# Between output projection and FFN1: another order of the norm chain of each token tile, its transposes one product sooner, the first operands split under the last product

## The chip, the cores and the metric

The kernel runs on one core of a Trainium2 chip. The metric is the device time of one execution in microseconds (us). The engines are named as the profile names them: PE is TensorE, DVE is VectorE, ACT is ScalarE, POOL is GpSimd, SP is SyncE, which here only issues transfers.

## The reference

One decoder layer for 512 prompt tokens and 64 sample tokens, D_MODEL 1024, D_FF 2816. The change lies in the second half of it:

```
m = merged @ w_out                              # merged: the gated sum of both branches
h = x + rms_norm(m, norm_mix_post)
f = swiglu(rms_norm(h, norm_ffn_pre))           # swiglu(h): a, u = split(h @ w_ffn_in); silu(a) * u @ w_ffn_out
y = h + rms_norm(f, norm_ffn_post)

rms_norm(x, w) = x * rsqrt(mean(x * x) + EPS) * w
```

Everything is float32. A float32 product is made on PE of three passes over rounded operands, so each operand x is split: hi = round(x), done as a copy (on ACT or POOL), and lo = x - hi, done on DVE.

## The kernel before, in words

The program is written out by hand: each engine has its own function (`@block.tensor`, `@block.vector`, `@block.scalar`, `@block.gpsimd`, `@block.sync`) and runs its instructions in the order written. Semaphores alone tie them together. An engine that waits holds up all that stands behind the wait in its own order.

The 576 tokens are five tiles c: 0 to 3 of 128 tokens, and NC (number 4) of 64. The output projection makes m in two halves of 512 columns. Each half of a tile is 4 weight units (UB to UB+3 for the first half, UB+4 to UB+7 for the second) of 2 row blocks of 3 passes: 24 matmuls (`out_part`, L342). The second half of tiles 0 and 1 is nearly done beforehand, with one unit left for each; of tiles 2, 3 and NC all 24 are done in the loop over c.

Each tile then goes through a **norm chain** that passes three times between the engines:

- ACT `out_square(1, c)` (L1223): square of the second half and its sum along the row; then `root` (L1228, L1230) for 1/rms of m. Signals m_sq, then m_rms.
- DVE `half_gain(1, c)` (L1416) after m_sq, then after m_rms two instructions that give h (L1445, L1447). Signals m_half and h_s. Below, these three are called new h.
- ACT `h_square(c)` (L1240, then L1228, L1230): 1/rms of h. Signals h_rms.
- DVE `normed(c)` (L1421): the normed tile in the buffer hn, which has three places (c % 3). Signals hn_s.
- PE `turn(c)` (L1606): eight transposes into two PSUM banks. Signals h_turn.
- ACT `x_copy(c)` (L1246): copy to `mt`, features by tokens. Signals x_tok.

FFN1 is computed by Strassen's scheme on 2 x 2 blocks: seven products m1 to m7 for each of 22 column blocks i, each of 12 matmuls (`do_product`, L1662, 288 columns). Their left operands are quarters of the turned h (a11, a12, a21, a22) or sums of them: s1 = a21 + a22, s2 = s1 - a11, s3 = a11 - a21, s4 = a12 - s2. Tokens 0 to 287 are a11 and a12; 288 to 575 are a21 and a22. The first XM = 224 columns of a sum need tiles up to 3 only ("main"); the last 64 need tile NC ("rest"). Before the first product with an operand, ACT makes its hi part (L1250, L1277) and DVE its lo part (`operand_lo`, L1405). The hi and lo parts of a11 and a12 lie in the buffers x_hi and x_lo, over operands of the output projection. The right operands are weight groups g0 to g3; the first five are copied by POOL (L1208, list `FIRST`), of these (1, g0) and (0, g1) after the whole output projection, and get their lo parts on DVE (`group_lo`, L1390). `weight_sums(1)` (L1397, L1399, L1401) makes the weight sums of i = 1.

`PAIR_ORDER` sets the order of the products on PE. Products m1 and m2 of an i share a bank: m2 is added to m1 there, and it may start only when ACT `front(i)` (L1269) has copied m1 out. After the products, DVE adds the results up (L1480: `upper_sum`, `lower_sum`, `lower_right` and so on), and from there on PE, ACT and DVE go in step through the i.

The loop that the change touches on PE is, before:

```
            ins.then_inc(out_done, 1)
            if c >= 2:
                turn(c - 2)
        turn(3)
```

## Time and profile before

| what | value |
|---|---|
| median of 3 runs | 1115.4 us (1114.63 to 1115.46) |
| profiled execution, its own time | 1116.85 us |
| profiled execution, its span | 1115.1 us |
| mean granted PE clock | 0.991 |
| busy: PE, DVE, ACT, POOL | 1077.2, 685.7, 480.1, 52.2 us |
| the stretch that the change touches | about 680 to 731 us of the span |

The profile gives for each engine how long it was busy, and for each idle stretch before an instruction what ended it. Busy time of PE is nearly the whole span, so an idle stretch on PE is what can be won. A timeline row shows start, duration and instruction; instructions on one engine overlap by some hundredths to tenths of a us, so the step from one to the next is the distance of their starts.

### The profile page before, as it was taken

The numbers are of one execution on the slowest core, as the hardware profiler recorded it, in microseconds if no ns is written. First come the engines' busy times: TensorE is split into PE (matmuls) and PEld (weight loads), VectorE is DVE, ScalarE is ACT, GpSimd is POOL, SyncE is SP. The second block draws the span as 40 slices with busy tenths as digits, with TensorE's granted clock in tenths as the row PEclk, the third lists the DMA queues.
The fourth block names the chain that finished last, engine by engine and source line by source line (L and its number), as shares of the span: only waits on it lengthen the run. The fifth ranks groups of instructions, "written<-read, shape, count | busy, mean of one in ns | idle before, by whom it ended". The sixth has DMA issues, their size and how long they took to land.

```text
span 1115.1 us, 25037 instructions
## 1 busy us (share of the span) xinstructions
PE 1077.2 (97%) x10956; PEld 1013.4 (91%) x10956; DVE 685.7 (61%) x1001; ACT 480.1 (43%) x765; POOL 52.2 (5%) x78
## 2 busy tenths in 40 slices
PE   4999999999999999999999998789999999999998
PEld 4999999999999999999999877689999999988886
DVE  4246543566533756345755376799999999844544
ACT  4252244532435432446234444654444444533532
POOL 6000000100001000011000101000000000000000
PEclk9999999999999999999999998999999999999999
DMA  6522232522224522235222083032424242322212
GB/s 166 147 77 69 67 86 85 163 78 67 70 66 133 152 59 77 68 98 168 62 75 77 30 266 83 9 106 77 114 77 114 76 115 76 114 95 90 81 57 85
DMA packets 138620, 105.20 MB, mean 94 GB/s; under 512 B 3968, under 2 KB 123776, under 8 KB 138512
## 3 DMA queue, kind: packets, MB, share of 16 engines
q1 hardware_dynamic: 133648, 85.78, 26.9%
q0 software_dynamic: 4864, 17.83, 5.2%
q8 instruction: 87, 1.43, 0.5%
q14 instruction: 21, 0.17, 0.1%
HBM read 91.79 MB, written 11.80 MB: 93 GB/s over the span
## 4 chain that ended last, share of the span: by engine, by line
PE 91%; DVE 4%; ACT 1%; DVEq 1%; ACTq 1%; issue 0%; POOL 0%; DMA 0%; POOLq 0%
PE ps L253 43%; PE ps L1662 19%; PE ps L1684 13%; PE ps L342 4%; PE ps L934 2%; PE ps L988 2%; PE ps L965 1%; PE ps L955 1%; PE ps L911 1%; PE ps L967 1%; PE ps L972 1%; PE ps L948 1%; PE ps L981 1%; PE ps L974 1%; PE ps L930 0%
## 5 line engine op out<-in xcount | busy, mean ns | idle before, releaser
L253 PE MATMUL ps<-x_hi,w_lo_t 128*128 128x288 f32 x1168 | 256.6, 301 | 4.5 <-DVE w_lo_t L243 4.5
L253 PE MATMUL ps<-x_hi,w_hi_t 128*128 128x288 f32 x1168 | 250.5, 296 | 0.0
L253 PE MATMUL ps<-x_lo,w_hi_t 128*128 128x288 f32 x1168 | 250.5, 296 | 0.0
L239 ACT ACTIVATE w_hi_t<-w_raw_t 128x1024 fp32r<-128x1024 f32 x73 | 77.2, 1058 | 334.0 <-PE ps L253 322.2
L243 DVE TENSOR_TENSOR w_lo_t<-w_raw_t,w_hi_t 128x1024 fp32r<-128x1024 f32 x75 | 91.7, 1222 | 187.1 <-ACT w_hi_t L239 187.1
L253 PEld LDWEIGHTS ps<-x_hi,w_lo_t 128*128 128x128 f32 x1168 | 187.4, 189 | 9.5 <-DVE w_lo_t L243 4.6
L253 PEld LDWEIGHTS ps<-x_lo,w_hi_t 128*128 128x128 f32 x1168 | 188.7, 189 | 0.0
L253 PEld LDWEIGHTS ps<-x_hi,w_hi_t 128*128 128x128 f32 x1168 | 188.7, 189 | 0.0
L1662 PE MATMUL ps<-x_hi,w_lo_t 128*128 128x288 f32 x264 | 78.7, 298 | 5.6 <-issue 4.2
L1662 PE MATMUL ps<-x_lo,w_hi_t 128*128 128x288 f32 x264 | 78.4, 297 | 0.0
L1662 PE MATMUL ps<-x_hi,w_hi_t 128*128 128x288 f32 x264 | 78.3, 297 | 0.0
L1285 ACT ACTIVATE w_hi_t<-merged 128x1024 fp32r<-128x1024 f32 x41 | 43.1, 1055 | 57.0 <-PE ps L1662 49.2
L731 DVE TENSOR_TENSOR Q<-Q,B 128x768 f32<-128x768 f32 (+1 forms) x24 | 23.8, 992 | 69.6 <-PE ps L934 30.2
L1684 PE MATMUL ps<-w_hi_t,x_hi 128*128 128x512 f32 x180 | 57.1, 389 | 0.0
L1480 DVE TENSOR_TENSOR work<-work,ps 128x288 f32<-128x288 f32 x110 | 49.7, 452 | 11.9 <-PE ps L1662 7.6
L1662 PEld LDWEIGHTS ps<-x_hi,w_lo_t 128*128 128x128 f32 x264 | 50.0, 190 | 6.3 <-issue 5.2
L1390 DVE TENSOR_TENSOR w_lo_t<-merged,w_hi_t 128x1024 fp32r<-128x1024 f32 x43 | 52.3, 1221 | 0.9
L1662 PEld LDWEIGHTS ps<-x_hi,w_hi_t 128*128 128x128 f32 x264 | 50.2, 190 | 0.0
L1662 PEld LDWEIGHTS ps<-x_lo,w_hi_t 128*128 128x128 f32 x264 | 50.1, 190 | 0.0
L1509 DVE TENSOR_TENSOR w_lo_t<-w_raw_t,w_hi_t 128x1024 fp32r<-128x1024 f32 x17 | 20.8, 1224 | 44.0 <-ACT w_hi_t L1324 44.0
L810 DVE SCALAR_TENSOR_TENSOR h_t<-h_t,dec,ps 128x128 f32<-128x128 f32 (+1 forms) x96 | 30.5, 387 | 18.6 <-PE ps L988 18.6
L1324 ACT ACTIVATE w_hi_t<-w_raw_t 128x1024 fp32r<-128x1024 f32 x17 | 18.0, 1059 | 54.7 <-PE ps L1684 50.3
(282 smaller groups left out, 2126.5 us busy)
## 6 DMA issues: line engine op xcount, KB each, us to landing
w_raw_t<-in_w_in_dram SPq DMA_DIRECT2D x73, 512.0 KB, 3.6
merged<-in_w_ffn_in_dram SPq DMA_DIRECT2D x22, 512.0 KB, 5.1
w_raw_t<-in_w_ffn_in_dram SPq DMA_DIRECT2D x22, 512.0 KB, 4.5
w_raw_t<-in_w_ffn_out_dram SPq DMA_DIRECT2D x22, 512.0 KB, 3.6
h_t<-in_x_prompt_dram SPq DMA_DIRECT2D x8, 512.0 KB, 6.2
h_t<-in_state_gla_dram POOLq DMA_DIRECT2D x4, 1024.0 KB, 6.1
h_t<-in_state_hgrn_dram POOLq DMA_DIRECT2D x8, 512.0 KB, 8.2
out_dram<-h_t POOLq DMA_DIRECT2D x4, 1024.0 KB, 5.3
```

Of the source, the lines that this page charges most:

```text
L239: nc.scalar.activation(w_hi_t[:, u % NSPL, 0:nk, :], w_raw_t[:, u % NRAW, 0:nk, :], ACT.Copy).then_inc(w_hi, 1)
L243: nc.vector.tensor_tensor(w_lo_t[:, u % NSPL, 0:nk, :], w_raw_t[:, u % NRAW, 0:nk, :], w_hi_t[:, u % NSPL, 0:nk, :].bitcast(F32), ALU.subt ...
L253: m = nc.tensor.matmul(out[:, q, :], w[:, u % NSPL, k, :], x(k, q), start=first and i == 0, stop=last and i == len(todo) - 1)
L342: ins = pe.matmul(out_bank(half, c), x[:, k, cols], w[:, kk, :], start=first and i == 0, stop=last and i == 2, skip_group_check=True)
L731: dve.tensor_tensor(qf, qf, first.broadcast_to(shape), ALU.mult)
L810: ins = dve.scalar_tensor_tensor(st, st, dec[:, h, NC + b:NC + b + 1], s[:, o:o + w], ALU.mult, ALU.add)
L934: m = nc.tensor.matmul(s[t:t + STRIP, o + t // 2:o + (t + STRIP) // 2], K[:, h, c * C + t:c * C + t + STRIP], second(Q[:, h, c * C + t:c * ...
L1285: act.activation(group(i, g, True), group_raw(i, g), ACT.Copy).then_inc(g_hi, 1)
L1390: dve.tensor_tensor(group(i, g, False), group_raw(i, g), group(i, g, True).bitcast(F32), ALU.subtract).then_inc(first_lo if (i, g) in FIRS ...
L1480: return dve.tensor_tensor(out, term, bank(i, m), ALU.add)
L1662: ins = nc.tensor.matmul(bank(i, m), w[:, k0 + k, :], xx[:, k, :], start=(k == 0 and n == 0 and m in STARTS), stop=(k == 3 and n == 2), sk ...
L1684: m = nc.tensor.matmul(f_bank(half, t), x, w, start=first and i == 0, stop=last and i == len(todo) - 1)
```

## The change

Nothing is computed that was not computed before, but for one instruction: ACT's copy for the hi part of s2 is made in two (main and rest). What changes is the order on three engines.

- PE: `turn(1)` and `turn(2)` both stand before the products of tile NC, `turn(3)` behind product (0, m1), `turn(NC)` behind (1, m1). In PAIR_ORDER (0, m2) now comes ahead of (1, m1). The matmuls of units UB+4 and UB+5 of tile NC signal a new semaphore x_free, since after them x_hi and x_lo of a11 and a12 are free.
- DVE: new h of tiles 0 and 1 come first, then `normed` of both; `group_lo(0, "g3")` and `weight_sums(1)` stand behind tiles 2 and 3; the lo parts of a11 and a12 are made ahead of new h of tile NC; s3 is made whole and after the lo part of s2; s4 after it.
- ACT: the roots and squares of tiles follow that order; the hi parts of a11 and a12 wait for x_free and stand ahead of tile NC's root.

```diff
--- before.py
+++ after.py
@@ -74,7 +74,7 @@
 PRODUCTS = {"m1": ("a11", "b11"), "m2": ("a12", "b21"), "m3": ("s4", "b22"), "m4": ("a22", "t4"),
             "m5": ("s1", "t1"), "m6": ("s2", "t2"), "m7": ("s3", "t3")}
 TURN = ("m1", "m6", "m7", "m5", "m2", "m4", "m3")
-PAIR_ORDER = ([(0, "m1"), (1, "m1"), (0, "m2"), (1, "m2")] + [(i, m) for i in (0, 1) for m in TURN if m not in ("m1", "m2")]
+PAIR_ORDER = ([(0, "m1"), (0, "m2"), (1, "m1"), (1, "m2")] + [(i, m) for i in (0, 1) for m in TURN if m not in ("m1", "m2")]
               + [(i, m) for i in range(2, FT) for m in TURN])
 PRODUCT_NO = {im: r for r, im in enumerate(PAIR_ORDER)}
 BANK = {"m1": 0, "m2": 0, "m5": 1, "m3": 1, "m6": 2, "m7": 3, "m4": 3}
@@ -1091,6 +1091,8 @@
     g_hi = sem("g_hi")
     g_lo = sem("g_lo")
     a_hi = sem("a_hi")
+    s_main = sem("s_main")
+    x_free = sem("x_free")
     s_rest = sem("s_rest")
     xs_hi = sem("xs_hi")
     xs_lo = sem("xs_lo")
@@ -1249,19 +1251,6 @@
             act.drain()
             act.activation(operand(x, True), x_raw[x], ACT.Copy).then_inc(a_hi, 1)
 
-        for i in range(NT):
-            if i >= 1:
-                h_square(i - 1)
-            if i >= 2:
-                x_copy(i - 2)
-            out_square(1, i)
-            root(i, part[0:tok(i), 1, i:i + 1], stat[0:tok(i), 0, i:i + 1], m_rms)
-        first_x_hi("a11")
-        h_square(NC)
-        x_copy(3)
-        first_x_hi("a12")
-        x_copy(4)
-
         def front(i):
             act.wait_ge(product, PRODUCT_NO[i, "m1"] + 1)
             if i >= 2:
@@ -1291,9 +1280,35 @@
                 act.wait_ge(act_s, i)
             act.activation(fs, fa[:, i % 2, :], ACT.Sigmoid).then_inc(sig_s, 1)
 
+        def h_root(c):
+            out_square(1, c)
+            root(c, part[0:tok(c), 1, c:c + 1], stat[0:tok(c), 0, c:c + 1], m_rms)
+
+        h_root(0)
+        h_root(1)
+        h_square(0)
+        h_square(1)
+        h_root(2)
+        x_copy(0)
+        h_square(2)
+        h_root(3)
+        x_copy(1)
+        x_copy(2)
+        h_square(3)
+        act.wait_ge(x_free, 1)
+        first_x_hi("a11")
+        act.wait_ge(x_free, 2)
+        first_x_hi("a12")
+        h_root(NC)
+        x_copy(3)
         front(0)
+        h_square(NC)
         front(1)
-        sum_hi(1, "s2")
+        x_copy(4)
+        act.wait_ge(s_main, 1)
+        act.activation(operand("s2", True)[:, :, 0:XM], sums["s2"][:, :, 0:XM], ACT.Copy)
+        act.wait_ge(s_rest, 1)
+        act.activation(operand("s2", True)[:, :, XM:HT], sums["s2"][:, :, XM:HT], ACT.Copy).then_inc(xs_hi, 1)
         sum_hi(2, "s3")
         sum_hi(1, "s1")
         act.activation(operand("a22", True), x_raw["a22"], ACT.Copy).then_inc(xs_hi, 1)
@@ -1425,20 +1440,16 @@
         dve.wait_ge(st_out, 80 * G)
         for c in range(NT):
             half_gain(0, c, m_half0[0:tok(c), c, :], m_zero)
-        group_lo(0, "g3")
-        dve.drain()
-        weight_sums(1)
-        for c in range(NT):
-            n, back = tok(c), hn[0:tok(c), c % 3, HALF:D]
-            if c == NC:
-                back = hn[0:n, 1, HALF:D]
-            if c >= 1:
-                normed(c - 1)
+
+        def second_sum(c):
+            n = tok(c)
+            return hn[0:n, c % 3, HALF:D]
+
+        def new_h(c):
+            n, back = tok(c), second_sum(c)
             if c >= 3:
                 dve.wait_ge(h_turn, c - 2)
             half_gain(1, c, back, m_half)
-            if c == NC:
-                group_lo(1, "g0")
             dve.wait_ge(h_in[c], 16)
             dve.drain()
             dve.wait_ge(m_rms, c + 1)
@@ -1446,34 +1457,47 @@
                                      ALU.mult, ALU.add)
             dve.scalar_tensor_tensor(h_t[0:n, c, HALF:D], back, stat[0:n, 1, c:c + 1], h_t[0:n, c, HALF:D],
                                      ALU.mult, ALU.add).then_inc(h_s, 1)
-            if c == 0:
-                dve.wait_ge(g_pre_in, 16)
-
+
+        def x_sum(x, a, op, b, cols):
+            return dve.tensor_tensor(sums[x][:, :, cols], a[:, :, cols], b[:, :, cols], op)
+        main, rest, whole = slice(0, XM), slice(XM, HT), slice(0, HT)
+
+        new_h(0)
+        new_h(1)
+        dve.wait_ge(g_pre_in, 16)
+        normed(0)
+        normed(1)
+        new_h(2)
+        group_lo(0, "g3")
+        normed(2)
+        new_h(3)
+        dve.drain()
+        weight_sums(1)
+        normed(3)
         dve.wait_ge(a_hi, 1)
         operand_lo("a11")
-        normed(NC)
         dve.wait_ge(a_hi, 2)
         operand_lo("a12")
-        main, rest = slice(0, XM), slice(XM, HT)
-
-        def x_sum(x, a, op, b, cols):
-            return dve.tensor_tensor(sums[x][:, :, cols], a[:, :, cols], b[:, :, cols], op)
+        new_h(NC)
+        group_lo(1, "g0")
+        normed(NC)
         dve.wait_ge(x_tok, NC)
-        for cols in (main, rest):
-            if cols == rest:
-                dve.wait_ge(x_tok, NT)
-            x_sum("s1", x_raw["a21"], ALU.add, x_raw["a22"], cols)
-            dve.drain()
-            s2 = x_sum("s2", sums["s1"], ALU.subtract, x_raw["a11"], cols)
-            s3 = x_sum("s3", x_raw["a11"], ALU.subtract, x_raw["a21"], cols)
-        s2.then_inc(s_rest, 1)
-        s3.then_inc(s_rest, 1)
+        dve.drain()
+        x_sum("s1", x_raw["a21"], ALU.add, x_raw["a22"], main)
+        dve.drain()
+        x_sum("s2", sums["s1"], ALU.subtract, x_raw["a11"], main).then_inc(s_main, 1)
         group_lo(0, "g1")
-        for k, x in enumerate(("s2", "s3", "s1")):
-            dve.wait_ge(xs_hi, k + 1)
+        dve.wait_ge(x_tok, NT)
+        x_sum("s1", x_raw["a21"], ALU.add, x_raw["a22"], rest)
+        dve.drain()
+        x_sum("s2", sums["s1"], ALU.subtract, x_raw["a11"], rest).then_inc(s_rest, 1)
+        dve.wait_ge(xs_hi, 1)
+        operand_lo("s2")
+        x_sum("s3", x_raw["a11"], ALU.subtract, x_raw["a21"], whole).then_inc(s_rest, 1)
+        dve.tensor_tensor(sums["s4"], x_raw["a12"], sums["s2"], ALU.subtract).then_inc(s_rest, 1)
+        for k, x in enumerate(("s3", "s1")):
+            dve.wait_ge(xs_hi, k + 2)
             operand_lo(x)
-            if x == "s3":
-                dve.tensor_tensor(sums["s4"], x_raw["a12"], sums["s2"], ALU.subtract).then_inc(s_rest, 1)
 
         def add_up(i, m, out, term):
             dve.wait_ge(product, PRODUCT_NO[i, m] + 1)
@@ -1634,10 +1658,14 @@
             for u in range(UB + 7 if c < 2 else UB + 4, UC):
                 for kk in range(2):
                     ins = out_part(nc.tensor, u, c, kk, u == UB + 4 and kk == 0, kk == 1)
+                if c == NC and u < UB + 6:
+                    ins.then_inc(x_free, 1)
             ins.then_inc(out_done, 1)
-            if c >= 2:
-                turn(c - 2)
-        turn(3)
+            if c == 2:
+                turn(0)
+            if c == 3:
+                turn(1)
+                turn(2)
 
         def do_product(i, m):
             x, b = PRODUCTS[m]
@@ -1666,6 +1694,8 @@
         for i, m in PAIR_ORDER:
             do_product(i, m)
             if (i, m) == (0, "m1"):
+                turn(3)
+            if (i, m) == (1, "m1"):
                 turn(NC)
 
         def tile(n, t, kks, first, last):
```

PE at the turns and the first product of FFN1 (ident is the identity matrix, so those rows are the transposes; each opening row of a product is shown). Before, in the order of the program, and each row once:

```order
L1606 MATMUL ps<-ident,a 128x128 [waits hn_s]
L1606 MATMUL ps<-ident,a 128x128 x7
L1606 MATMUL ps<-ident,a 128x128 [waits x_tok,hn_s]
L1606 MATMUL ps<-ident,a 128x128 x7
L1662 MATMUL ps<-x_hi,w_lo_t 128x288 [waits x_tok,m_half,xs_lo,first_lo]
L1662 MATMUL ps<-x_lo,w_hi_t 128x288
```

and with the change, between the products of tile 3 and those of tile NC:

```order
L342 MATMUL ps<-xe_hi,x_hi 128x512
L1630 MATMUL ps<-ident,a 128x128 [waits hn_s]
L1630 MATMUL ps<-ident,a 128x128 x7
L1630 MATMUL ps<-ident,a 128x128 [waits hn_s]
L1630 MATMUL ps<-ident,a 128x128 x7
L342 MATMUL ps<-xe_lo,x_hi 128x512 [waits m_zero]
```

Before, turn(2) and turn(3) stood between tile NC's products and (0, m1). Now turn(1) and turn(2) stand ahead of tile NC's products, and (0, m1) follows those at once.

DVE from the first half's gains on, before:

```order
L1416 TENSOR_TENSOR work<-ps,a 64x512 [waits m_sq]
L1390 TENSOR_TENSOR w_lo_t<-merged,w_hi_t 128x1024 [waits first_hi]
L1397 TENSOR_TENSOR merged<-w_raw_t 128x1024 [waits pair_raw1]
L1399 TENSOR_TENSOR merged<-w_raw_t,merged 128x512
L1401 TENSOR_TENSOR merged<-w_raw_t,merged 128x512
L1416 TENSOR_TENSOR a<-ps,a 128x512 [waits m_sq]
L1445 SCALAR_TENSOR_TENSOR h_t<-work,stat,h_t 128x512 [waits h_in0,m_rms]
L1447 SCALAR_TENSOR_TENSOR h_t<-a,stat,h_t 128x512
L1421 SCALAR_TENSOR_TENSOR a<-h_t,stat,a 128x1024 [waits h_rms,g_pre_in]
```

and with the change:

```order
L1431 TENSOR_TENSOR work<-ps,a 64x512 [waits m_sq]
L1431 TENSOR_TENSOR a<-ps,a 128x512 [waits m_sq]
L1456 SCALAR_TENSOR_TENSOR h_t<-work,stat,h_t 128x512 [waits h_in0,m_rms]
L1458 SCALAR_TENSOR_TENSOR h_t<-a,stat,h_t 128x512
L1431 TENSOR_TENSOR a<-ps,a 128x512 [waits m_sq]
L1456 SCALAR_TENSOR_TENSOR h_t<-work,stat,h_t 128x512 [waits h_in1,m_rms]
L1458 SCALAR_TENSOR_TENSOR h_t<-a,stat,h_t 128x512
L1436 SCALAR_TENSOR_TENSOR a<-h_t,stat,a 128x1024 [waits h_rms,g_pre_in]
L1436 SCALAR_TENSOR_TENSOR a<-h_t,stat,a 128x1024 [waits h_rms]
```

The four weight instructions no longer stand ahead of tile 0, and tile 1's new h is done while ACT makes tile 0's root.

DVE from tile 3's last step to the lo part of s3, with the change (before, the lo part of a12 stood behind normed(NC), and all six sums ahead of the first lo part):

```order
L1436 SCALAR_TENSOR_TENSOR a<-h_t,stat,a 128x1024 [waits h_rms]
L1420 TENSOR_TENSOR x_lo<-a,x_hi 128x1152 [waits a_hi] x2
L1431 TENSOR_TENSOR a<-ps,a 64x512 [waits m_sq,h_turn]
L1456 SCALAR_TENSOR_TENSOR h_t<-work,stat,h_t 64x512 [waits h_in4,m_rms]
L1458 SCALAR_TENSOR_TENSOR h_t<-a,stat,h_t 64x512
L1405 TENSOR_TENSOR w_lo_t<-w_raw_t,w_hi_t 128x1024 [waits first_hi]
L1436 SCALAR_TENSOR_TENSOR a<-h_t,stat,a 64x1024 [waits h_rms]
L1462 TENSOR_TENSOR a<-a 128x4x224 [waits x_tok]
L1462 TENSOR_TENSOR a<-a 128x4x224
L1405 TENSOR_TENSOR w_lo<-merged,w_hi 128x512 [waits first_hi]
L1462 TENSOR_TENSOR a<-a 128x4x64 [waits x_tok]
L1462 TENSOR_TENSOR a<-a 128x4x64
```

Both lo parts (one row, x2) now come ahead of tile NC, and one sum fewer stands ahead of the rest sums in each part.

## Rows read from the trace of the kernel before

**Rows 1.** The page, its part 1, the engines over the whole span
```profile
PE 1077.2 (97%) x10956; PEld 1013.4 (91%) x10956; DVE 685.7 (61%) x1001; ACT 480.1 (43%) x765; POOL 52.2 (5%) x78
```

**Rows 2.** Engines by stretch of 2 us: busy time, then PEclk, DMA share, GB/s
```profile
690.00:692.00 2.00, 1.85 (x9) 1.85 (x10) 1.91 (x4) 0.00 (x0) 0.00 (x0) 0.50 0.02 4
...
714.00:716.00 2.00, 2.00 (x10) 2.00 (x10) 1.28 (x1) 1.90 (x2) 0.00 (x0) 0.50 0.00 0
...
722.00:724.00 2.00, 0.35 (x3) 0.11 (x1) 1.70 (x3) 2.00 (x3) 0.00 (x0) 1.00 0.04 11
```

**Rows 3.** Timeline, PE: start us, us, line, instruction, [idle before <- releaser]
```profile
686.31 0.40 PE L342 MATMUL ps<-xe_hi,x_hi 128*128 128x512 f32 x1
...
690.15 1.97 PE L1606 MATMUL ps<-ident,a 128*128 128x128 f32 x8 [3.44 <-DVE a L1421]
...
699.37 1.03 PE L1606 MATMUL ps<-ident,a 128*128 128x128 f32 x8
...
705.83 1.03 PE L1606 MATMUL ps<-ident,a 128*128 128x128 f32 x8
...
708.23 1.09 PE L1606 MATMUL ps<-ident,a 128*128 128x128 f32 x8 [1.36 <-DVE a L1421]
...
713.55 0.58 PE L1662 MATMUL ps<-x_hi,w_lo_t 128*128 128x288 f32 x1 [4.23 <-issue]
...
724.38 0.37 PE L1662 MATMUL ps<-xe_hi,w_lo_t 128*128 128x288 f32 x1 [2.04 <-issue]
...
730.54 0.37 PE L1662 MATMUL ps<-x_hi,w_lo_t 128*128 128x288 f32 x1 [0.52 <-DVE work L1480]
```

**Rows 4.** The chain of waits in order of time, its piece from 754.49 us (asked up to 810 us)
```profile
754.49 55.54 PE ps L1662 x417
```

**Rows 5.** Timeline, ACT: the norm chain, the copies, the first halves
```profile
679.76 0.60 ACT L1223 ACTIVATE a<-ps 128x512 f32<-128x512 f32 x1 [1.03 <-PE ps L342]
...
680.26 0.19 ACT L1223 ACTIVATION_READ_ACCUMULATOR a<-ps 128x1 f32 x1
...
680.90 0.20 ACT L1230 ACTIVATE stat<-stat 128x1 f32<-128x1 f32 x1
...
686.92 1.06 ACT L1240 ACTIVATE a<-h_t 128x1024 f32<-128x1024 f32 x1 [5.82 <-DVE h_t L1447]
...
693.92 1.00 ACT L1246 ACTIVATE a<-ps 128x1024 f32<-128x1024 f32 x1
...
715.13 1.16 ACT L1250 ACTIVATE x_hi<-a 128x1152 fp32r<-128x1152 f32 x1
...
717.88 0.40 ACT L1269 ACTIVATE work<-ps 128x288 f32<-128x288 f32 x1
```

**Rows 6.** Timeline, DVE: from the weight sums to the first product sum
```profile
681.87 1.23 DVE L1397 TENSOR_TENSOR merged<-w_raw_t 128x1024 f32<-128x1024 f32 x1
...
684.69 0.69 DVE L1416 TENSOR_TENSOR a<-ps,a 128x512 f32<-128x512 f32 x1
...
688.81 1.28 DVE L1421 SCALAR_TENSOR_TENSOR a<-h_t,stat,a 128x1024 f32<-128x1024 f32 x1 [1.92 <-ACT stat L1230]
...
706.27 1.90 DVE L1421 SCALAR_TENSOR_TENSOR a<-h_t,stat,a 128x1024 f32<-128x1024 f32 x1 [1.85 <-ACT stat L1230]
...
716.32 1.36 DVE L1405 TENSOR_TENSOR x_lo<-a,x_hi 128x1152 fp32r<-128x1152 f32 x1 [1.01 <-ACT x_hi L1250]
...
728.12 0.46 DVE L1480 TENSOR_TENSOR work<-work,ps 128x288 f32<-128x288 f32 x1
```

**Rows 7.** Groups of DVE instructions, shapes apart, 716 to 732 us
```profile
L1460 DVE TENSOR_TENSOR a<-a 128x896 f32<-128x896 f32 x3 | 3.2, 1087 | 0.1
...
L1460 DVE TENSOR_TENSOR a<-a 128x256 f32<-128x256 f32 x3 | 1.2, 421 | 0.1
```

**Rows 8.** Timeline, POOL: its two copies after the output projection
```profile
706.06 1.04 POOL L1208 CAST w_hi_t<-w_raw_t 128x1024 fp32r<-128x1024 f32 x1 [32.70 <-PE ps L342]
...
707.04 1.60 POOL L1208 CAST w_hi<-merged 128x512 fp32r<-128x512 f32 x1
```

## The prediction

> **What bounds the kernel now.** I read the page first: PE is busy 1077.2 of 1115.1 us [rows 1], so time can be won only where PE stands idle or runs at the lower clock. Next the timeline of PE around the change. It shows five holes [rows 3]: 3.44 us ahead of turn(0) at 690.15, 1.36 ahead of turn(3) at 708.23, 4.23 ahead of (0, m1) at 713.55, 2.04 ahead of (0, m6) at 724.38, and 0.52 ahead of (0, m4) at 730.54. That is 11.6 us. Then the windows for the clock: after the first and the third hole the granted clock is 0.50, the lower level of 1.2 GHz [rows 2]. After the hole of 2.04 us it was still 1.00 [rows 2]. Last, the timelines of ACT and DVE tell what each hole waits for. PE is not short of work there: it waits for the norm chain of a tile, which DVE (weight sums first) and ACT hand to and fro. From 754.49 us on PE runs on without a hole [rows 4], so a shift of all engines that lasts until there lasts to the end.
>
> **The change, part by part.** All times are on the span of the profiled execution.
>
> *Turn(0).* PE is through tile 2's products at 686.55 (686.31 and one step of 0.24) and stands until 690.15 [rows 3], because DVE did the weight sums from 681.87 on and came to tile 0's new h only at 684.69 [rows 6]. Its new h takes until 686.92, 2.23 us with the hand-over, and the root and the next start on DVE come 1.89 later, at 688.81 [rows 5, 6]. With the change DVE has no weight work ahead. ACT's square of tile 0 starts at 679.76, its row sum is there at 680.45 and its root at 681.10 [rows 5]. So new h of tile 0 runs from 680.5 to 682.8, that of tile 1 until 684.9 (its root, 1.34 behind the same product order, is there at 682.5), and normed(0), 1.28 long, ends at 686.1. ACT is through with tile 0's root of h at 684.6. Turn(0) starts at once at 686.55, with 0.4 us to spare. The hole of 3.44 us goes, and with it the slow stretch behind it.
>
> *Tile 3.* A turn and the 24 matmuls of a tile at full clock are 705.83 - 699.37 = 6.46; the turn's share is about 0.8 (1.03 less the overlap with the next) [rows 3]. Tile 3 is done at 686.55 + 6.46 = 693.0; before it was 699.4. PE has gained 6.4 us there. Turn(1) and turn(2) follow without a wait: normed(2) ends at about 693.4 by the same steps, turn(2) is due at 693.8. Tile NC's products run 694.6 to 700.3.
>
> *From here DVE sets the pace.* It has nearly no idle time in the following sum, which starts from tile 3's result at 693.15.
> - Row sum of the square: 0.69 [rows 5], with hand-over 693.95. New h(3): 2.23, to 696.2.
> - Weight sums: 2.82 (681.87 to 684.69) [rows 6], to 699.0. They were in front of tile 0 before; now (0, m1) waits for them.
> - normed(3): 1.20 (1.28 less the overlap with the next), to 700.2. ACT has tile 3's root long before, at 698.2 (behind two copies of 1.00 each [rows 5]).
> - Lo part of a11: 1.36 [rows 6], step 1.28, to 701.5. Its hi part on ACT is 1.16 [rows 5] and done at 699.4, since x_free came at 696.1. **(0, m1) starts at 701.6** instead of 713.55, after a hole of 1.3 us.
> - Lo part of a12: 1.28, plus POOL. POOL's copies for (1, g0) and (0, g1) come now at 700.4, when the output projection ends. Before, they met normed(3), which took 1.90 instead of 1.28 [rows 6], and POOL's own half-size copy took 1.60 [rows 8]. I take the 0.62 that DVE lost: to 703.4.
> - New h(NC) 2.2, to 705.6. The lo part of (1, g0) lies under ACT's root. The root is there 1.89 later, at 707.5. normed(NC), to 708.7.
> - s1 and s2 main: 1.09 each [rows 7], to 711.0. Lo part of (0, g1) 0.6. s1 and s2 rest 0.42 each [rows 7], with their waits to 712.4. ACT's rest copy, about 0.4 (as the 128x288 copy [rows 5]) to 712.9. Lo part of s2 1.36, to 714.3. **(0, m6) starts at 714.4** instead of 724.38.
> - s3 and s4: 1.27 each. Lo part of s3, to 718.2, **(0, m7) at 718.3**. Lo part of s1, to 719.5.
> - The first product sum starts on DVE at 719.5. Before, it was 728.12 [rows 6].
>
> On the POOL term the Trainium skill, page "SBUF — State Buffer", has a harder rule in its section "Who interferes with whom": a DVE instruction with two SBUF inputs and a GpSimd one exclude each other for the whole instruction. The trace agrees so far as normed(3) lost 0.62 to the end of a copy and the next copy lost about 1.1 to it; the rule's consequence here is a rival below.
>
> *What PE does meanwhile.* A product is 12 matmuls of 55.54/417 = 0.133 us [rows 4], 1.6 us. (0, m1) to 703.2, turn(3) to 704.0. Then (0, m2) needs ACT's copy of m1: ACT first copies tile 3 (1.00), then m1 (0.40) [rows 5], so PE waits about 1.6 us, to 705.7. This wait is new; before, (1, m1) lay there. (0, m2), (1, m1), turn(NC) and (1, m2) end at 711.3. Then a hole of 3.1 us before (0, m6), and one of 2.3 us after it before (0, m7), which is new too: before, s3 was ready together with s2. Holes are again some 8 us together. None of the holes of PE is on the path by itself, except as DVE is late. So the 12 us gained at (0, m1) shrink to 10 at (0, m6) and to 8.6 at the first product sum.
>
> *Behind it* the order of DVE and ACT is the same as before, and so are the sizes; PE's last three small holes up to 754.49 come from DVE, which is full there. The weight transfers for i = 2 start on the lo part of (0, g1), which is itself 10 us earlier. The shift passes on whole. The extra copy on ACT costs one start of an instruction and lies under DVE's work: nothing.
>
> *The sum.* 728.12 - 719.5 = 8.6. Adding up the kernel before with the same steps from 684.69 gives 726.9 for its 728.12: hand-overs are worth 1.2 more than I count. The stretch with the change has somewhat fewer of them, and I take 0.7. **The gain is 7.9 us.** Against the profiled execution: span 1115.1 - 7.9 = 1107.2, time 1116.85 - 7.9 = 1108.95. That execution was 1.45 above the median of the three runs, so for a median I say 1115.4 - 7.9 = **1107.5 us**. Without further mishap 1106.5 to 1108.5 (hand-overs 0 to 1.5, POOL 0 to 0.6).
>
> **The rivals.**
>
> *Both POOL copies block DVE whole.* The whole copy is 1.04 [rows 8], the one of half the size half of that, and both then stand in DVE's chain: 1.5 us instead of 0.62. For it: [rows 6, 8], where the two together took longer than each alone. Against: DVE's queue is full there, and POOL may be the one to wait, as at 707.04. Time 1108.4. That is also what the rule of the Trainium skill, page "SBUF — State Buffer", would make of it if POOL comes first both times.
>
> *The clock falls in the two holes before (0, m6) and (0, m7).* Before, 3.44 and 4.23 us of waiting were followed by 0.50 and 2.04 were not [rows 2, 3]; 3.1 and 2.3 with one product between lie in the middle. (0, m6) at half clock ends at 717.6, still ahead of 718.3. (0, m7) and (0, m5) lose 1.6 each as long as it lasts; DVE needs (0, m7) at 721.1 and (0, m5) at 722.7, so 0.1 to 2.5 of the 3.2 reach the path. Time about 1109, up to 1110.
>
> *Tile 0 misses its turn.* The margin is 0.4 us. If DVE or ACT lose a us or two on the first two tiles, the hole at turn(0) remains in part and the clock may go with it; the gain at tile 3 falls from 6.4 to some 3, and less weight work is hidden. Time 1110.5 to 1113. Against it: each step has a row.
>
> *More is kept.* If POOL costs nothing and the hand-overs are as short as I count, 1106; if besides the lo part of s3 comes without the wait on ACT's hi part, 1105.5.
>
> *Slower: the clock does not come back.* The new order has four holes (1.3, 1.6, 3.1, 2.3) with never more than some 6 us of work between. If the clock falls in the first and stays at 0.50 through (1, m7), that is 11 products at 3.2 instead of 1.6 and two turns, 19 us more of PE's time. Adding 3.2 per product and 1.6 per turn from 701.6 on, PE reaches (0, m4) at 728.4, still 2.1 ahead of before, for the new holes are then filled. (0, m4), (0, m3), (1, m6) and (1, m7) lose 6.4, so (1, m7) ends 4.3 later than before: about 1119. It decides from the point where the slow clock outlasts (0, m4). Against it: the clock that was at 0.50 at 690 gave a turn of 1.03 instead of 1.97 by 699.37, and turn(3), behind the hole of 1.36, took 1.09, the full-clock time [rows 2, 3].
>
> **How the numbers follow.** A measurement of this kernel can tell a difference of about 0.2%, 2.2 us. Forecast (1106.5 to 1108.5): 0.58. POOL blocks whole: 0.10. Clock falls in the pair of holes: 0.18. More kept: 0.05. Tile 0 misses its turn: 0.06, of which a third would end within 2.2 us of before. Slower: 0.03. So faster 0.95, same 0.02, slower 0.03. The range of 8 in 10 takes in the forecast, POOL and most of the clock case: 1105.9 to 1110.2.
>
> **What would show it.** Right: no hole on PE ahead of turn(0) and the clock at 1.00 from 688 to 700 us; (0, m1) at about 702 and waiting for the lo part of a11; new holes ahead of (0, m2) (released by ACT), (0, m6) and (0, m7) (by DVE); DVE without idle time from 694 to 719 but for three short waits; the first product sum at about 720. Wrong: a hole ahead of turn(0) or of turn(2); a clock of 0.50 anywhere from 700 to 725; a distance from (0, m4) to the end of the span that is not the 384.6 us of before [rows 3], which would mean that the shift is not passed on.

## The result, and the profile after

| | before | changed |
|---|---|---|
| median of 4 runs each, compared on one chip | 1115.43 us (1114.63 to 1116.64) | 1107.64 us (1106.44 to 1108.25) |
| ratio, with its 95% interval | | 0.9928 [0.9911, 0.9945] |
| profiled execution, span | 1115.1 us | 1105.5 us |

The change takes 7.8 us off. The forecast was 1107.5. The page shows no change of PE's share, only that its busy time fell by 4.9 us, from 1077.2 [rows 1], for the same number of matmuls (x10956); fewer of them ran at the lower clock. DVE has one instruction fewer, since s3 is made whole, and ACT one more, the second copy of s2:

```profile
PE 1072.3 (97%) x10956; PEld 1008.4 (91%) x10956; DVE 685.3 (62%) x1000; ACT 480.7 (43%) x766; POOL 53.1 (5%) x78
```

The spans differ by 9.6 us, not by 7.8. ACT's square of tile 0's second half, which lies ahead of anything that the change touches, starts at 679.76 before [rows 5] and here at 678.47, 1.29 us earlier. Starts of this instruction lie between 678.4 and 680.1 in all traces of this case, whatever the kernel, so that part is scatter of what runs ahead of it. I therefore measure from it: **D** is the distance from that start to the first product sum on DVE. It is 728.12 - 679.76 = 48.36 before [rows 5, 6] and 718.49 - 678.47 = 40.02 after, **8.34 less**. To compare single times with the forecast, add 1.29.

The timeline of PE after; it answers to [rows 3]:

```profile
685.25 1.03 PE L1630 MATMUL ps<-ident,a 128*128 128x128 f32 x8
...
691.70 1.91 PE L1630 MATMUL ps<-ident,a 128*128 128x128 f32 x16
...
700.34 0.37 PE L1690 MATMUL ps<-x_hi,w_lo_t 128*128 128x288 f32 x1 [1.15 <-issue]
...
702.01 1.03 PE L1630 MATMUL ps<-ident,a 128*128 128x128 f32 x8
...
704.55 0.37 PE L1690 MATMUL ps<-x_hi,w_lo_t 128*128 128x288 f32 x1 [1.51 <-ACT work L1258]
...
713.43 0.58 PE L1690 MATMUL ps<-xe_hi,w_lo_t 128*128 128x288 f32 x1 [3.03 <-issue]
...
717.29 0.37 PE L1690 MATMUL ps<-xe_hi,w_lo 128*128 128x288 f32 x1 [0.64 <-issue]
...
720.91 0.37 PE L1690 MATMUL ps<-x_hi,w_lo_t 128*128 128x288 f32 x1 [0.20 <-DVE work L1504]
```

There is no hole ahead of turn(0) (685.25), nor ahead of turn(1) and turn(2), which are one row of 16 transposes at 691.70. (0, m1) waits 1.15 us, (0, m2) 1.51, (0, m6) 3.03, (0, m7) 0.64. The last row is (0, m4): from its start to the end of the span it is 384.6 us (1105.5 - 720.91), as before.

The windows after: busy time of PE, PEld, DVE, ACT, POOL, then the granted clock, DMA share and GB/s:

```profile
688.00:690.00 2.00, 2.00 (x10) 1.64 (x9) 1.94 (x3) 1.15 (x2) 0.00 (x0) 1.00 0.02 4
...
702.00:704.00 2.00, 1.04 (x10) 0.81 (x8) 1.88 (x4) 0.92 (x1) 0.82 (x1) 1.00 0.00 0
...
714.00:716.00 2.00, 2.00 (x11) 2.00 (x10) 2.00 (x3) 1.36 (x2) 0.00 (x0) 0.50 0.90 236
...
718.00:720.00 2.00, 2.00 (x17) 2.00 (x16) 1.97 (x3) 1.55 (x3) 0.00 (x0) 1.00 0.00 0
```

After turn(0) the clock stays at 1.00, where it was 0.50 before [rows 2]. Between turn(0) and (0, m4) it is 0.50 once, from about 713.3 to 716.8 by windows of 1 us, from the end of the hole ahead of (0, m6) until (0, m6) is through.

The timeline of DVE after; it answers to [rows 6]:

```profile
683.48 1.28 DVE L1436 SCALAR_TENSOR_TENSOR a<-h_t,stat,a 128x1024 f32<-128x1024 f32 x1
...
690.66 1.28 DVE L1436 SCALAR_TENSOR_TENSOR a<-h_t,stat,a 128x1024 f32<-128x1024 f32 x1 [0.72 <-ACT stat L1232]
...
692.69 0.69 DVE L1431 TENSOR_TENSOR a<-ps,a 128x512 f32<-128x512 f32 x1 [0.75 <-ACT a L1225]
...
694.98 1.23 DVE L1412 TENSOR_TENSOR merged<-w_raw_t 128x1024 f32<-128x1024 f32 x1
...
697.69 1.28 DVE L1436 SCALAR_TENSOR_TENSOR a<-h_t,stat,a 128x1024 f32<-128x1024 f32 x1
...
698.89 3.46 DVE L1420 TENSOR_TENSOR x_lo<-a,x_hi 128x1152 fp32r<-128x1152 f32 x2
...
706.43 1.28 DVE L1436 SCALAR_TENSOR_TENSOR a<-h_t,stat,a 64x1024 f32<-64x1024 f32 x1 [0.72 <-ACT stat L1232]
...
711.97 1.36 DVE L1420 TENSOR_TENSOR xe_lo<-a,xe_hi 128x1152 fp32r<-128x1152 f32 x1 [0.48 <-ACT xe_hi L1311]
...
718.49 0.46 DVE L1504 TENSOR_TENSOR work<-work,ps 128x288 f32<-128x288 f32 x1
```

normed(0) starts at 683.48 instead of 688.81. From tile 3's half gain (692.69) on, DVE waits only for the root of tile NC (0.72 us at 706.43) and for the rest copy of s2 (0.48 us at 711.97). Two lo parts in one row take 3.46 us at 698.89, where 2.64 would be the step and duration of two of them. The answer for this line alone gives the duration of one, min, median and max in ns: the 2194 is the second of the pair, and it is the collision with POOL, below.

```profile
L1420 DVE TENSOR_TENSOR x_lo<-a,x_hi x4: 1350/1352/2194, 698.9 to 718.9; 128x1152 fp32r<-128x1152 f32 x4
```

ACT and POOL after; they answer to [rows 5] and [rows 8]:

```profile
678.47 0.60 ACT L1225 ACTIVATE a<-ps 128x512 f32<-128x512 f32 x1 [1.03 <-PE ps L342]
...
704.00 0.41 ACT L1258 ACTIVATE work<-ps 128x288 f32<-128x288 f32 x1
...
704.61 1.06 ACT L1242 ACTIVATE a<-h_t 64x1024 f32<-64x1024 f32 x1 [0.20 <-DVE h_t L1458]
```

```profile
699.25 1.89 POOL L1210 CAST w_hi_t<-w_raw_t 128x1024 fp32r<-128x1024 f32 x1 [27.42 <-PE ps L342]
...
701.09 1.73 POOL L1210 CAST w_hi<-merged 128x512 fp32r<-128x512 f32 x1
```

### The profile page after: what moved, and what is told of

The parts are those of the page before. It is cut to its first block, busy times and chain, and to the rows that moved or that the text cites. A ratio compares the mean times of both kernels' runs of the same rounds, so it can differ in the third digit from the quotient of the medians.

```text
span 1105.5 us, 25038 instructions
## 1 busy us (share of the span) xinstructions
PE 1072.3 (97%) x10956; PEld 1008.4 (91%) x10956; DVE 685.3 (62%) x1000; ACT 480.7 (43%) x766; POOL 53.1 (5%) x78
## 4 chain that ended last, share of the span: by engine, by line
PE 92%; DVE 4%; DVEq 1%; ACT 1%; POOL 0%; issue 0%; ACTq 0%; DMA 0%; POOLq 0%
PE ps L253 43%; PE ps L1690 20%; PE ps L1714 13%; PE ps L342 5%; PE ps L934 2%; PE ps L988 2%; PE ps L965 1%; PE ps L955 1%; PE ps L911 1%; PE ps L967 1%; PE ps L972 1%; PE ps L948 1%; PE ps L981 1%; PE ps L974 1%; PE ps L930 0%; POOL O L403 0%
## 5 line engine op out<-in xcount | busy, mean ns | idle before, releaser
L239 ACT ACTIVATE w_hi_t<-w_raw_t 128x1024 fp32r<-128x1024 f32 x73 | 77.3, 1058 | 333.7 <-PE ps L253 321.7
L1274 ACT ACTIVATE w_hi_t<-merged 128x1024 fp32r<-128x1024 f32 x41 | 43.1, 1055 | 57.0 <-PE ps L1690 49.2
L1690 PE MATMUL ps<-xe_hi,w_lo_t 128*128 128x288 f32 x128 | 38.5, 301 | 4.2 <-issue 3.0
```

Source lines behind the costliest of these rows:

```text
L239: nc.scalar.activation(w_hi_t[:, u % NSPL, 0:nk, :], w_raw_t[:, u % NRAW, 0:nk, :], ACT.Copy).then_inc(w_hi, 1)
L1274: act.activation(group(i, g, True), group_raw(i, g), ACT.Copy).then_inc(g_hi, 1)
L1690: ins = nc.tensor.matmul(bank(i, m), w[:, k0 + k, :], xx[:, k, :], start=(k == 0 and n == 0 and m in STARTS), stop=(k == 3 and n == 2), sk ...
```

## The experiments

All of them are measured by D and by a second distance. The hole on PE ahead of (2, m6), which DVE's lo part of a weight group ends, has the same 1.21 us in all traces. In the timeline of PE before and after it is this row:

```profile
744.94 0.40 PE L1662 MATMUL ps<-xe_hi,w_lo_t 128*128 128x288 f32 x1 [1.21 <-DVE w_lo_t L1390]
```

```profile
735.29 0.40 PE L1690 MATMUL ps<-xe_hi,w_lo_t 128*128 128x288 f32 x1 [1.21 <-DVE w_lo_t L1405]
```

From its end to the end of the span it is 370.1 to 370.3 us in all traces (1115.1 - 744.94 before, 1105.5 - 735.29 after). So, the scatter ahead of D aside, whatever a kernel wins or loses lies in D, or in the stretch between D's end and that matmul, called **S**. S is 16.82 before and 16.80 after. D and S come from one trace of each kernel. The ratio is to the kernel before as it ran beside each group of kernels (medians 1115.43, 1115.67, 1115.60 and 1115.33 us).

| kernel | D | S | median us | ratio to before, interval |
|---|---|---|---|---|
| before | 48.36 | 16.82 | 1115.4 | |
| changed | 40.02 | 16.80 | 1107.64 | 0.9928 [0.9911, 0.9945] |
| changed, again | 40.01 | 18.55 | 1108.90 | 0.9937 [0.9925, 0.9950] |
| weights later only | 43.89 | 16.81 | 1111.91 | 0.9964 [0.9950, 0.9978] |
| split late | 45.60 | 18.73 | 1114.87 | 0.9993 [0.9984, 1.0003] |
| split late, square first | 44.99 | 17.70 | 1113.07 | 0.9980 [0.9970, 0.9990] |
| old product order | 40.02 | 17.70 | 1108.29 | 0.9935 [0.9917, 0.9952] |
| sums whole | 39.84 | 16.82 | 1107.02 | 0.9922 [0.9906, 0.9938] |
| one more DVE instruction | 41.18 | 18.17 | 1110.83 | 0.9960 [0.9948, 0.9972] |
| weight sums last | 42.07 | 16.81 | 1110.43 | 0.9956 [0.9944, 0.9969] |
| fill | 39.43 | 16.80 | 1107.61 | 0.9930 [0.9918, 0.9942] |
| copies off POOL | 39.70 | 17.67 | 1108.32 | 0.9937 [0.9925, 0.9949] |
| three edits | 38.46 | 16.82 | 1106.34 | 0.9921 [0.9909, 0.9932] |
| three edits, sums split | 37.89 | 16.81 | 1105.75 | 0.9908 [0.9893, 0.9923] |

**Weights later only.** The kernel before, with one part of the change.

```diff
-        group_lo(0, "g3")
-        dve.drain()
-        weight_sums(1)
         for c in range(NT):
...
             if c == 0:
                 dve.wait_ge(g_pre_in, 16)
+            if c == 2:
+                group_lo(0, "g3")
+            if c == 3:
+                dve.drain()
+                weight_sums(1)
```

> The kernel before, with one part of the change alone: on VectorE the lo part of (0, g3) and the weight sums of i = 1 stand behind new h of tiles 2 and 3 instead of ahead of tile 0. I measure D, from the start of ACT's square of tile 0's second half to the first product sum on DVE (before 48.36 us, changed kernel 40.02 us). My theory (the hole at turn(0) comes from the weight work, and DVE paces the rest): no hole ahead of turn(0), no clock of 0.50 behind it, a new hole of some 2 to 3 us ahead of turn(3), (0, m1) some 6 us earlier than before, D about 42.4, time 6 us under the kernel before. Rival (the order of the turns and the early split carry most of the gain): D 45 to 47, time at most 3 us under before.

D fell by 4.47, a little over half of the change's 8.34. The hole ahead of turn(0) is gone. The timeline of PE shows two holes of another kind, ahead of turn(3) and of (0, m1):

```profile
703.77 1.97 PE L1608 MATMUL ps<-ident,a 128*128 128x128 f32 x8 [3.82 <-DVE a L1421]
...
708.56 0.58 PE L1664 MATMUL ps<-x_hi,w_lo_t 128*128 128x288 f32 x1 [2.82 <-issue]
```

The 3.82 us cost the clock as well: it was 0.50 from about 702.2 to 712.5 us, (0, m1) included. D lies between the two theories (42.4 and 45 to 47), and the median, 3.8 us under its kernel before (1115.67), between them too. What I had missed is POOL: its copies met the weight sums here, which took 1.23, 1.35 and 0.92 us instead of 1.23, 0.69 and 0.69. That is 0.89 of the 1.5 us above 42.4; the rest is not accounted for. So the order of the weights alone is worth somewhat more than half. The turns and the early split make up the rest, by difference: no run moves the turns by themselves.

**Split late.** The changed kernel, with the first operands split behind tile NC's root and new h again.

```diff
-        act.wait_ge(x_free, 1)
-        first_x_hi("a11")
-        act.wait_ge(x_free, 2)
-        first_x_hi("a12")
         h_root(NC)
+        act.wait_ge(x_free, 1)
+        first_x_hi("a11")
+        act.wait_ge(x_free, 2)
+        first_x_hi("a12")
...
-        dve.wait_ge(a_hi, 1)
-        operand_lo("a11")
-        dve.wait_ge(a_hi, 2)
-        operand_lo("a12")
         new_h(NC)
         group_lo(1, "g0")
+        dve.wait_ge(a_hi, 1)
+        operand_lo("a11")
+        dve.wait_ge(a_hi, 2)
+        operand_lo("a12")
```

> The changed kernel with a11 and a12 split late again: hi parts behind tile NC's root on ACT, lo parts behind new h(NC) and the lo part of (1, g0) on DVE. My theory: ACT's root of h(NC) stands behind its copy of (0, m1), so normed(NC) and all sums wait for (0, m1): (0, m1) starts 4 to 5 us later, D 44.0 instead of 40.02, time 4 us over the changed kernel. Rival (only the total of DVE's work between tile 3 and the first product sum counts, whatever its order): D 39.5 to 40.0, time the same.

D grew by 5.58, the time by 6 to 7 us (against the two medians of the changed kernel, 1108.90 and 1107.64). On PE the hole ahead of (0, m1) is 5.52 us, with the clock at 0.50 behind it (the first matmul 0.58 us long, as at 713.55 in [rows 3]):

```profile
706.02 0.58 PE L1690 MATMUL ps<-x_hi,w_lo_t 128*128 128x288 f32 x1 [5.52 <-issue]
```

and on DVE normed(NC) then waits 6.13 us for ACT's root of h, which stands behind ACT's copy of (0, m1):

```profile
713.31 1.28 DVE L1436 SCALAR_TENSOR_TENSOR a<-h_t,stat,a 64x1024 f32<-64x1024 f32 x1 [6.13 <-ACT stat L1232]
```

So the total of DVE's work is not what counts: DVE idles here. The miss of 1.6 against 44.0 is the clock. (0, m1) and turn(3) lie ahead of ACT's root of h(NC); from (0, m1) to turn(3) it was 3.01 instead of 1.67 us, and turn(3) took 1.22 instead of 1.03. The kernel lost this although it had one thing for free: POOL's two copies were through before the lo parts began (at 704.58), and these took 2.61 us instead of 3.46.

**Split late, square first.** As the last, with one more edit on ACT.

```diff
+        h_square(NC)
         x_copy(3)
         front(0)
-        h_square(NC)
```

> The kernel with the late split (D 45.60), and on ACT the square of h(NC) ahead of the copy of turned tile 3 and of (0, m1)'s copy. My theory (late splitting costs because PE's (0, m1) and turn(3) lie in the path of the sums, through ACT's order and through the copy of tile 3): normed(NC) comes 4 us earlier or more, but s1 main then waits for the copy of tile 3, which follows (0, m1); D 42.9. Rival (only the clock and the square's place cost): D 40 to 40.5.

The edit did what it says, and normed(NC) came early, at 706.78. But D fell by 0.61 only. The timeline of DVE shows where the wait went:

```profile
706.78 1.27 DVE L1436 SCALAR_TENSOR_TENSOR a<-h_t,stat,a 64x1024 f32<-64x1024 f32 x1
...
711.43 2.26 DVE L1462 TENSOR_TENSOR a<-a 128x896 f32<-128x896 f32 x2 [3.38 <-ACT a L1248]
...
716.51 0.93 DVE L1462 TENSOR_TENSOR a<-a 128x256 f32<-128x256 f32 x2 [2.22 <-ACT a L1248]
```

s1 main waits 3.38 us for the copy of turned tile 3, as expected, and then s1 rest waits 2.22 us for the copy of tile NC, which turn(NC) follows only behind (1, m1). I had forgotten the second. Both turns stand behind a product on PE; so long as (0, m1) is late, all sums are late. That is why mending ACT's order alone wins back so little. D is 2.1 above the 42.9 worked out, and most of this is the clock once more: from (0, m1) to turn(3) it was 3.02 us instead of 1.67, and turn(3) took 1.56 instead of 1.03, 1.9 us together. Without it D would be about 43.1, an estimate from these rows, which is what my theory gave, and far from the rival's 40 to 40.5.

**Old product order.** The changed kernel with PAIR_ORDER as before.

```diff
-PAIR_ORDER = ([(0, "m1"), (0, "m2"), (1, "m1"), (1, "m2")] + ...
+PAIR_ORDER = ([(0, "m1"), (1, "m1"), (0, "m2"), (1, "m2")] + ...
```

> The changed kernel with the old order of the first products: (0, m1), turn(3), (1, m1), turn(NC), (0, m2), (1, m2). My theory (DVE paces, PE's holes there are not on the path): the hole of 1.5 us ahead of (0, m2) goes and one of about 3 us ahead of (1, m1) comes, since its weights' lo part is late; (0, m6) starts at the same distance, D 40.0 within 0.2, time the same as the changed kernel. Rival (the order of the products is worth its hole): D 1.5 us away, either way.

D is 40.02 to the hundredth, though PE's holes moved: 2.71 us ahead of (1, m1) for its weights' lo part, 1.57 ahead of (0, m6), 2.04 ahead of (0, m7).

```profile
705.83 0.40 PE L1690 MATMUL ps<-x_hi,w_lo_t 128*128 128x288 f32 x1 [2.71 <-DVE w_lo_t L1405]
...
713.50 0.37 PE L1690 MATMUL ps<-xe_hi,w_lo_t 128*128 128x288 f32 x1 [1.57 <-issue]
...
717.36 0.37 PE L1690 MATMUL ps<-xe_hi,w_lo 128*128 128x288 f32 x1 [2.04 <-issue]
```

In D this part of the change is worth nothing by itself: the product order only chooses where PE waits. S is 17.70, 0.9 more than in the first trace of the changed kernel, with the clock at 0.50 from about 718.0 to 721.4, while (0, m7) and (0, m5) ran. Whether the order has a part in that is not shown, since S of the changed kernel itself differs by more than this between two traces.

**Sums whole.** The changed kernel with the sums and the hi part of s2 as before.

```diff
-        act.wait_ge(s_main, 1)
-        act.activation(operand("s2", True)[:, :, 0:XM], sums["s2"][:, :, 0:XM], ACT.Copy)
-        act.wait_ge(s_rest, 1)
-        act.activation(operand("s2", True)[:, :, XM:HT], sums["s2"][:, :, XM:HT], ACT.Copy).then_inc(xs_hi, 1)
+        sum_hi(1, "s2")
```

(and DVE's loop over main and rest of s1, s2, s3, as in the kernel before)

> The changed kernel with the sums as before: s1, s2, s3 main, then all three rest, and the hi part of s2 in one piece. My theory: (0, m6) starts about 1 us later, (0, m7) follows it without a hole, and D stays within 0.3 of 40.02, since DVE does the same work; time the same as the changed kernel. Rival (starting (0, m6) early is part of the gain): D and the time 1 to 2 us longer.

(0, m6) started 1.15 us later, (0, m7) without a hole, D 0.18 less. The finer cut of the sums brings nothing either; by trace it is a little worse.

**One more DVE instruction.** The changed kernel with s1 main computed twice.

```diff
         x_sum("s1", x_raw["a21"], ALU.add, x_raw["a22"], main)
+        dve.drain()
+        x_sum("s1", x_raw["a21"], ALU.add, x_raw["a22"], main)
```

> The changed kernel with s1 main computed twice: one more DVE instruction of 1.09 us, with its wait 1.2 us, ahead of (0, m6), at a place where PE has a hole of 3.0 us. My theory (DVE paces): D 41.2, time 1.2 longer. Rival (PE's holes have slack): D 40.0, time the same.

D grew by 1.16, by just the instruction and its wait. PE's hole ahead of (0, m6) grew by as much and gave nothing of it away:

```profile
715.45 0.58 PE L1692 MATMUL ps<-xe_hi,w_lo_t 128*128 128x288 f32 x1 [4.20 <-issue]
```

So DVE sets the pace from normed(NC) on. The median grew by 3.2 or 1.9 us (against 1107.64 and 1108.90), more than D, and S tells why: it is 18.17, 1.37 more, with the clock at 0.50 from about 713.5 to 723.7 (below).

**Weight sums last.** The changed kernel with `weight_sums(1)` behind the lo part of s1.

```diff
         new_h(3)
-        dve.drain()
-        weight_sums(1)
         normed(3)
...
             operand_lo(x)
+        weight_sums(1)
```

> The changed kernel with the weight sums of i = 1 (2.8 us of DVE) moved from ahead of normed(3) to behind the lo part of s1. My theory: in their old place they lie partly under ACT's root of tile 3 (DVE would idle some 2 us there), so (0, m1) starts only 0.8 us earlier, the 2.8 us come back later, and D grows by about 2, to 42.0; time 2 us over the changed kernel. Rival (they stand in the way of (0, m1), and what starts earlier there ends earlier): D 37.2, time 2.8 under it.

D 42.07, as worked out, 2 us worse. normed(3) waits for ACT's root of tile 3 in their stead:

```profile
698.16 1.28 DVE L1436 SCALAR_TENSOR_TENSOR a<-h_t,stat,a 128x1024 f32<-128x1024 f32 x1 [2.10 <-ACT stat L1232]
```

The place behind new h(3) is thus a good one: 2.1 of their 2.7 us lie under ACT's work.

**Fill.** The changed kernel with the lo part of (0, g1) in DVE's wait for the root of tile NC.

```diff
         group_lo(1, "g0")
+        group_lo(0, "g1")
         normed(NC)
...
         x_sum("s2", sums["s1"], ALU.subtract, x_raw["a11"], main).then_inc(s_main, 1)
-        group_lo(0, "g1")
```

> The changed kernel with the lo part of (0, g1) moved on DVE into its wait of 0.72 us ahead of normed(NC). My theory (DVE paces from tile 3 to the first product sum, so filled idle time is time won): D 39.4 instead of 40.02, time 0.6 us shorter, which the runs can hardly tell but the trace can. Rival (PE paces): D unchanged.

D 39.43: 0.59 won, as expected, and not to be told in the medians.

**Copies off POOL.** The changed kernel; POOL makes its copy for (0, g1) with its first ones, and ACT that for (1, g0).

```diff
-        for i, g in FIRST:
+        for i, g in ((0, "g2"), (0, "g0"), (0, "g3"), (0, "g1")):
             if (i, g) == (0, "g0"):
                 pool.wait_ge(unit_done, UB + 3)
-            if (i, g) == (1, "g0"):
-                pool.wait_ge(out_done, 2 * NT)
...
         h_root(NC)
+        act.wait_ge(pair_raw[1], 32)
+        act.activation(group(1, "g0", True), group_raw(1, "g0"), ACT.Copy).then_inc(first_hi, 1)
         x_copy(3)
...
-                dve.wait_ge(first_hi, FIRST[i, g])
+                dve.wait_ge(first_hi, FIRST[i, g] if i == 0 and g != "g1" else FIRST_GROUPS)
```

> The changed kernel without POOL's two copies behind the output projection: ACT makes the one for (1, g0) while it waits for turn(3), and POOL makes that for (0, g1) 30 us earlier, where DVE idles. My theory (the lo part of a12 took 2.19 instead of 1.35 us because POOL's copy shut DVE out): all lo parts take 1.35, D 39.2, time 0.8 shorter. Rival (the 2.19 has another cause, such as PE or ACT reading the same buffers): the lo part of a12 stays at 2.2, D 40.0.

The cause is shown, the gain only in part. POOL's copy for (0, g1), which now meets nothing, and DVE after the edit:

```profile
673.02 0.61 POOL L1208 CAST w_hi<-merged 128x512 fp32r<-128x512 f32 x1
```

```profile
699.91 2.62 DVE L1420 TENSOR_TENSOR x_lo<-a,x_hi 128x1152 fp32r<-128x1152 f32 x2
...
707.13 1.28 DVE L1436 SCALAR_TENSOR_TENSOR a<-h_t,stat,a 64x1024 f32<-64x1024 f32 x1 [1.24 <-ACT stat L1230]
```

The two lo parts take 2.62 instead of 3.46 us. But normed(NC) now waits 1.24 instead of 0.72 us, for the root on ACT, which runs behind the copies of tile 3 and of (0, m1) and so hangs on PE. Only 0.32 of the 0.84 reached D, and none of it the median: S is 17.67, with the clock at 0.50 from about 719.1 to 722.5. Between (0, m1) and normed(NC) the loop PE, ACT, DVE is nearly as long as DVE's own work, so DVE paces there by 0.32 us only.

**Three edits.** Fill, copies off POOL, and s3 ahead of the lo part of s2, in DVE's wait of 0.48 us.

```diff
+        x_sum("s3", x_raw["a11"], ALU.subtract, x_raw["a21"], whole).then_inc(s_rest, 1)
         dve.wait_ge(xs_hi, 1)
         operand_lo("s2")
-        x_sum("s3", x_raw["a11"], ALU.subtract, x_raw["a21"], whole).then_inc(s_rest, 1)
```

> The changed kernel with three edits: the lo part of (0, g1) in DVE's wait ahead of normed(NC), the copies off POOL as in the run before last, and s3 made ahead of the lo part of s2, in DVE's wait of 0.48 us for ACT. My theory: D 40.02 - 0.6 - 0.84 - 0.48 = 38.1, time 1.9 us under the changed kernel, 1105.7 us. Rival (behind the first product sum PE and ACT pace, and a gain above some tenths is lost there): D 38.1, but (0, m4) to the end longer by what was won, time 1107.

D fell by 1.56 of the 1.92 worked out (38.46 against 38.1); of the three, the copies had brought 0.32 of their 0.84 when alone. S is 16.82, so all of it passed on.

**Three edits, sums split.** As the last, and the last weight sum moved into what is left of the wait ahead of normed(NC).

```diff
-        weight_sums(1)
+        weight_sums(1, (0, 1))
         normed(3)
...
         group_lo(0, "g1")
+        weight_sums(1, (2,))
         normed(NC)
```

> The kernel with the three edits (D 38.46), and the last of the three weight sums moved from ahead of normed(3) into DVE's remaining wait ahead of normed(NC). My theory: normed(3), both lo parts and (0, m1) come 0.6 us earlier, the moved sum fills idle time, D 37.9, time 0.6 under that kernel, 1105.7. Rival (that wait is gone already, or ACT's root of tile 3 sets normed(3)): D 38.4 or more.

D 37.89, S 16.81, median 1105.75 us (1104.44 to 1106.03). This version beats both kernels: 9.6 us under the kernel before it was compared with (1115.33), and 1.9 and 3.2 under the two medians of the changed one, 1107.64 and 1108.90. By trace it is 2.13 us of D under it.

**Changed, again.**

> The changed kernel once more, with no edit. Its trace gives D again and the distance from the first product sum to the first matmul of (2, m6), behind the hole of 1.21 us, which is 16.8 us where the clock stays at 1.00 there and 17.7 to 18.7 in runs in which it was at 0.50 while (0, m7) and its neighbours ran. My theory: D 40.0 within 0.1, and that distance is one of these, not fixed by the kernel; time 1107.6 within 0.8.

D is the same, S is 1.75 longer and so is the time from the first product sum to the end. The median, 1108.90, is 1.3 above the 1107.6 expected, outside the 0.8 allowed. The windows of this execution:

```profile
712.00:714.00 2.00, 0.59 (x2) 0.62 (x3) 2.00 (x2) 0.00 (x0) 0.00 (x0) 0.58 0.98 277
...
716.00:718.00 2.00, 1.36 (x6) 1.05 (x6) 2.00 (x2) 2.00 (x3) 0.00 (x0) 0.50 0.00 0
...
718.00:720.00 2.00, 2.00 (x10) 2.00 (x9) 1.97 (x3) 1.53 (x3) 0.00 (x0) 0.50 0.00 0
```

The clock was at 0.50 from about 712.3 to 722.6, through (0, m6), (0, m7) and nearly all of (0, m5), not only while (0, m6) ran.

## Why the prediction was right

On the scale of the kernel before (measured start plus 1.29):

| step | forecast | measured |
|---|---|---|
| turn(0) starts | 686.55 | 686.54 |
| tile 3 done, turn(1) starts | 693.0 | 692.99 |
| (0, m1) starts | 701.6 | 701.63 |
| (0, m2) starts | 705.7 | 705.84 |
| (0, m6) starts | 714.4 | 714.72 |
| (0, m7) starts | 718.3 | 718.58 |
| first product sum | 719.5 | 719.78 |

- *Turn(0)* was right: 3.44 us of hole and the slow stretch behind it are gone. "Weights later only" shows that the order of the weights by itself does this. The clock after the hole of 2.04 us was read rightly, though the third row of [rows 2] covers the hole and not what follows: the windows from 724 to 728 are 1.00 too.
- *From tile 3 on DVE sets the pace* was right in the number, and too simple as a sentence. Each instruction of the chain took its place as added up. "One more DVE instruction" confirms it from normed(NC) on. Before that, ACT's root of tile 3 ("weight sums last": 2 of 2.7 us of DVE work hidden) and the loop through (0, m1) ("copies off POOL": 0.32 of 0.84) bind almost as tightly. A sum along one engine came out right because in this order that engine has hardly a wait left.
- *The early split* stood in the sum only as times of (0, m1). Its worth is 5.6 us of D when undone, clock included. The two late-split runs show why: ACT's order puts the root of h(NC) behind (0, m1), and where that is mended the sums wait for turn(3) and turn(NC), which stand behind products. The prediction said that PE's holes are not on the path "except as DVE is late"; with the late split they are on it.
- *The POOL term* was mis-sized: I took 0.62, DVE lost 0.84 (3.46 against 2.62), and only 0.32 of that reaches D, since without it ACT's root of h(NC) ends last. The rival, 1.5 us with both copies blocking, did not come: the trace shows the second copy waiting for the lo part and then running beside an instruction with a PSUM operand, which took its usual 0.69 us. Its half-size copy was put at half of 1.04, 0.52; alone it takes 0.61.
- *The allowance for hand-overs*, 0.7, was too large: 719.78 against 719.5 is 0.28. By trace the gain is 8.34, not 7.9.
- *The clock rival* came, in the trace of the change and more in its repetition, and 0.18 looks too low a chance for it. With it came one of the three signs named for "wrong", a clock of 0.50 between 700 and 725; the other two, a hole ahead of turn(0) or turn(2) and a distance other than 384.6 us behind (0, m4), did not. Its mechanism and price were as forecast: (0, m6) at half clock was hidden by the wait for s3's lo part and cost nothing in the first trace (S 16.80); where the clock stayed down, 1.75 us were lost, within the 0.1 to 2.5 forecast. 8.34 - 1.75 = 6.6 is about the 6.4 us between the medians of the repetition and its kernel before (1108.90 and 1115.33), and 7.8 lies between 6.6 and 8.3. That the first median meets 1107.5 to 0.1 us is then partly luck, likely two errors of opposite sign: too much allowance for hand-overs, nothing for the clock. How often the clock stays down in unprofiled runs was not counted.
- *Passed on whole* was right, the clock aside: 370.1 to 370.3 us from (2, m6) to the end in every trace, and S is 16.80 to 16.82 in eight of the fourteen traces. The other six, 17.67 to 18.73, are the ones in which (0, m5) began at the clock of 0.50 (its first rows take 0.44 instead of 0.29 us).
- *The slower rival's* sum does not come out of its own words: seven products at 3.2 and two turns at 1.6 from 701.6 give 727.2, not 728.4, for (0, m4), unless part of the wait ahead of (0, m2) is added. The forecast does not use it.

## What to carry to other kernels

When three engines hand a chain to each other, add up the work of the one that is hardly ever idle, and fill each of its waits with work that is due later: here 2.1 us of weight sums cost nothing under another engine's root, and cost 2.05 us when moved behind the last lo part, where nothing is left to wait for. Work whose result is needed only later must not stand ahead of the first link of such a chain. If a step of the chain stands behind a large unit of another engine (a turn behind a product), that unit's start is on the path, however many holes the engine has.
